# Moving four convolution projections ahead of the third mixer's sigmoid tiles, with a later start of that mixer's chain

## What is computed

```
fc = heads(f_c, H_C)
kc = (1.0 - lbh) * jax.nn.sigmoid(-fc)
log_f = jnp.log1p(-jnp.minimum(kc, GATE_CLAMP))
hC, Sh1 = _gla_chunked(jax.nn.silu(heads(q_c, H_C)), kc, heads(i_c, H_C), log_f, Sh0)
yC = jax.nn.silu(g_c) * _head_rms(hC, norm_c)
yconv, buf1 = _short_conv(cg_d * x_d, buf0, conv_w)
yD = bg_d * yconv
```

## Time and profile before

| | us |
|---|---|
| median of 3 runs | 1595.56 (1595.1 to 1599.61) |
| the profiled execution's own time | 1595.64 |
| its span, first to last instruction | 1593.8 |
| PE busy | 1538.8 (97%) |
| POOL, DVE and ACT busy | 888.1, 996.3 and 666.0 |

### The profile page before, as it was taken

How to read it: one execution, slowest core, us unless ns; L and a number is a source line. 1 busy time by engine, 2 the same in 40 slices (tenths; PEclk the granted TensorE clock), 3 DMA queues, 4 the chain that set the end, 5 groups by cost and what they waited for, 6 DMA issues and landing times.

```text
span 1593.8 us, 26238 instructions
## 1 busy us (share of the span) xinstructions
PE 1538.8 (97%) x10442; PEld 1477.8 (93%) x10442; DVE 996.3 (63%) x1929; ACT 666.0 (42%) x1220; POOL 888.1 (56%) x381
## 2 busy tenths in 40 slices
PE   7899999999999999999888999999999999999996
PEld 7899998999999999999888999889999999999996
DVE  4874775237676777754447747752467767777544
ACT  5434443333444544433344444434344445444333
POOL 6456444444445666677654554444444556666674
PEclk9999999999999999999999999999999999999998
DMA  8333353443354444444433334433334444444442
GB/s 284 119 115 123 137 177 101 154 135 122 121 175 151 142 138 148 151 148 151 139 106 106 119 120 164 161 124 132 122 135 141 156 140 141 136 151 150 149 151 79
DMA packets 66257, 223.61 MB, mean 140 GB/s; under 512 B 8024, under 2 KB 12632, under 8 KB 66136
## 3 DMA queue, kind: packets, MB, share of 16 engines
q1 hardware_dynamic: 66136, 221.93, 43.3%
HBM read 206.33 MB, written 15.58 MB: 139 GB/s over the span
## 4 chain that ended last, share of the span: by engine, by line
PE 87%; DVE 7%; ACT 3%; issue 1%; POOL 1%; DMA 0%; DVEq 0%; ACTq 0%
PE gps L1284 25%; PE gps L1286 24%; PE gps L1285 24%; PE xp L1523 2%; PE xp L1525 1%; PE xp L1460 1%; DVE mix L981 1%; PE xp L1438 1%; PE xp L1419 1%; PE xp L1512 1%; PE xp L1429 1%; PE xp L1421 1%; POOL wlo L594 1%; PE xp L1408 1%; ACT whi L615 1%
## 5 line engine op out<-in xcount | busy, mean ns | idle before, releaser
L594 POOL TENSOR_TENSOR wlo<-raw,whi 128x1024 fp32r<-128x1024 f32 x362 | 875.7, 2421 | 687.2 <-ACT whi L615 413.2
L1284 PE MATMUL gps<-xh,whi 128*128 128x320 f32 (+1 forms) x2000 | 643.3, 322 | 29.7 <-DVE zc L854 12.0
L1285 PE MATMUL gps<-xl,whi 128*128 128x320 f32 (+1 forms) x2000 | 625.7, 313 | 0.0
L1286 PE MATMUL gps<-xh,wlo 128*128 128x320 f32 (+1 forms) x2000 | 624.9, 312 | 0.0
L615 ACT ACTIVATE whi<-raw 128x1024 fp32r<-128x1024 f32 x258 | 272.3, 1056 | 348.7 <-PE gps L1286 297.7
L1284 PEld LDWEIGHTS gps<-xh,whi 128*128 128x128 f32 x2000 | 381.3, 191 | 38.5 <-POOL wlo L594 19.3
L1285 PEld LDWEIGHTS gps<-xl,whi 128*128 128x128 f32 x2000 | 382.8, 191 | 3.4 <-issue 0.4
L1286 PEld LDWEIGHTS gps<-xh,wlo 128*128 128x128 f32 x2000 | 382.3, 191 | 0.0
L1284 PE MATMUL gps<-ah,whi 128*128 128x320 f32 x640 | 199.1, 311 | 0.6
L1286 PE MATMUL gps<-ah,wlo 128*128 128x320 f32 x640 | 197.8, 309 | 0.0
L1285 PE MATMUL gps<-al,whi 128*128 128x320 f32 x640 | 197.7, 309 | 0.0
(11 more groups left out here) (299 smaller groups left out, 1893.3 us busy)
## 6 DMA issues: line engine op xcount, KB each, us to landing
raw<-in_w SPq DMA_DIRECT2D x362, 512.0 KB, 3.5
s<-in_st SPq DMA_DIRECT2D x24, 512.0 KB, 4.3
out_ss<-s SPq DMA_DIRECT2D x24, 512.0 KB, 2.7
con<-in_cst SPq DMA_DIRECT2D x4, 526.0 KB, 5.9
out_sp<-pst SPq DMA_DIRECT2D x24, 64.0 KB, 2.6
mix<-in_x SPq DMA_DIRECT2D x4, 320.0 KB, 4.9
out_y<-mix SPq DMA_DIRECT2D x8, 160.0 KB, 1.9
ee<-in_cst SPq DMA_DIRECT2D x1, 224.0 KB, 4.4
```

What stands on the lines that cost most here:

```text
L594: nc.gpsimd.tensor_tensor(wlo[:, c % RING, :, :], raw[:, c % RING, :, :], whi[:, c % RING, :, :].bitcast(F32), ALU.subtract).then_inc(lo_d ...
L1284: M(out, hi, xhi, start=start, stop=False)
L1285: M(out, hi, xlo, start=False, stop=False)
L1286: return M(out, lo, xhi, start=False, stop=stop)
```

## The change

The four `cD` slots move from places 16 to 19 to places 4 to 7, and `fC`, `qC` and `gC` come four slots later (8 to 19); the packed weights follow the same list, so the DMAs move with them. All stages that are due by those slots move by four: `c_log` 12, 13; `c_first` 16 to 19; `c_level` 21, 23, 25, 27, 29, 31; `c_last` 33. The cost entry of `c_last` falls from 4 to 2, so that `num` follows it by two slots and not by four: `num` 35, 38, 41, 44 and `fin` 36, 39, 42. `fin` of the last head is placed ahead of slot 45, behind slot 44, where `num` of that head and `conv` of head 3 stand too, in the order `num`, `conv`, `fin`. `conv` keeps its slots, and so does everything from slot 45 on.

```
-    for kind in ("vC", "fC", "qC", "gC", "cD", "xD", "bD", "vA", "qA", "kA", "oA", "ifA"):
+    for kind in ("vC", "cD", "fC", "qC", "gC", "xD", "bD", "vA", "qA", "kA", "oA", "ifA"):
...
-COST = {"c_log": 1, "c_first": 1, "c_level": 2, "c_last": 4, "a_gate": 1, "a_cum": 1, "a_row": 2, "a_exp": 1,
+COST = {"c_log": 1, "c_first": 1, "c_level": 2, "c_last": 2, "a_gate": 1, "a_cum": 1, "a_row": 2, "a_exp": 1,
```

## The result

The changed kernel takes 1606.83 us (median of 5 runs, 1603.73 to 1609.74), the kernel before beside it 1595.56 (5 runs, 1595.08 to 1599.61). The ratio is 1.0065, 95% interval 1.0045 to 1.0085: slower by 0.65%, a small loss, but the interval leaves out one. The profiled execution took 1605.67, its span is 1603.9 us against 1593.8, 10.1 longer.

A forecast was written before the change was run, and what follows sets the result against it. PE, busy 1538.8 of 1593.8 us, was taken as the bound. 2 x (0.7 + 2.7 + 1.6) - 0.3 = +9.7 us on 1595.64 gave 1605.3, range 1599 to 1612.

The forecast's parts named there:

- The sigmoid run: Twelve sigmoid tiles in a row, four slots later: cost unchanged, save 0.3 us gained at layer 0's first gap.
- Levels 0 and 1: Slots beside these levels become `xD`, taken out by DVE: distances end late, +0.7 us a layer.
- `c_last` to `num`: `c_last`'s 9.86 us chain covered by two slots, 7.2 us, instead of four: PE waits 2.7 us a layer.
- The tail: Behind slot 44, `num`, `conv`, `fin` without slots between: +1.6 us a layer, including `a_cum`'s wait gone, -1.2.
- `num` to `fin`: Behind slot 44, `fin`'s matmuls wait for `num`'s last copies and `vm`: PE waits about 1.8 us a layer.
- `a_gate`: Behind slot 45, waits for all of `fin`, which ends 4.67 us into a slot covering 3.8: about 1.0 us a layer.
- SP's queue: Stores of `fin` and of head 3's `conv` ahead of slot 49's weights, needed four slots later: cost nothing.
- Clock: Two gaps removed, six added, about two drawing a lower-clock stretch: taken as zero, 3 us either way.
- the first (a meeting of `conv`): `conv` behind slot 44 meets POOL once: +4.2 us for both layers; with one more slow stretch, 1611; chance 0.14.
- the second (L1003 misses POOL): `c_last`'s last DVE product, L1003, does not meet POOL: 1601.1 us; chance 0.10.
- the third: Sigmoid run keeps ahead of PE; all 12.0 us of waits and a slow stretch go: 1591.8 us; chance 0.04.
- the fourth: DVE's chain behind `c_last` and in the tail shorter than bounded, all terms at low ends: 1598 us; chance 0.06.

The follow-up runs named there:

- the exchange: Changed kernel with `c_last`'s two last DVE products swapped, so the one `num` reads comes first: 1601.44 us, ratio 1.0019 to the kernel before.
- e2_cost_only: Kernel before, in its old order of projections, with only the cost of `c_last` lowered from 4 to 2: 1613.08 us, ratio 1.0098.
- e9_one_slot: Changed kernel with the cost of `c_last` at 1 instead of 2, one covering slot before `num`: 1633.07 us, ratio 1.0225 to the kernel before.
- e6_gate_late: Kernel before, costs kept, with `gC` moved behind `qA` and `c_first` beside `cD`: 1586.15 us, ratio 0.9941.
- e3_spread: Changed kernel with `c_last` cost 3 and `finC` cost 1, spreading `num` and `fin` evenly: 1599.47 us, ratio 1.001 to the kernel before.

## Why the prediction was right, and where it was off

1605.3 was forecast and 1606.83 came, in the range and with the sign. By its own steps, measured on the trace:

- **The sigmoid run** (-0.3 for both layers): held. The gaps 2.04, 0.83, 1.83, 1.81 came back four slots later, and layer 0's first one went from 2.37 to 2.04. With the gap that moved from L1453, the term is -0.4.
- **Levels 0 and 1** (+0.7 a layer): 0.2. Both copies met POOL as the step had it, but they were done sooner: the distances began 4.79 us after POOL did, where the step had 5.0 to 5.3, and the first took 0.68 instead of 0.8. So level 0 ended only some 0.2 us late. DVE around it, and POOL:

```profile
99.28 2.07 DVE L908 COPY ud<-cbs 128x16 f32<-128x16 f32 x1
101.86 1.85 DVE L908 COPY ud<-cbs 128x16 f32<-128x16 f32 x1
...
103.75 0.68 DVE L928 TENSOR_TENSOR mix<-zc 128x512 f32<-128x512 f32 x1
...
98.96 4.71 POOL L594 TENSOR_TENSOR wlo<-raw,whi 128x1024 fp32r<-128x1024 f32 x2 [2.60 <-ACT whi L615]
```

- **`c_last` to `num`** (+2.7): 2.70 and 2.69. The wait is chain less cover. It is so at one slot as well (6.22), and the exchange showed the meeting with POOL in it.
- **The tail**: `num` to `fin` +1.8 (its own rows give 160.78 less 159.11, 1.67), measured 1.71 in both layers; `a_gate` +1.0, measured 0.94 in layer 1 and hidden in layer 0; `a_cum` -1.2, gone in both. `conv` was harmless where it stands, as the step assumed. But the two experiments that moved it or left it alone say that this was one good place between bad ones.
- **SP's queue** ("they cost nothing"): this step failed in layer 0, 1.07 us. It looked at the weights of slot 49. Those that came late are slot 47's, behind the stores of `fin` of head 2, and the split of them on ACT stood ahead of the copy that L1438 reads. The timelines of SP's queue and of ACT, layer 0:

```profile
210.13 1.25 SPq L554 DMA_DIRECT2D out_sp<-pst  x1
211.44 0.45 SPq L535 DMA_DIRECT2D raw<-in_w  x1
...
215.76 1.06 ACT L615 ACTIVATE whi<-raw 128x1024 fp32r<-128x1024 f32 x1 [2.38 <-DMA raw<-in_w]
```

  In layer 1 the same store held the queue 0.43 us and not 1.25, ACT waited 1.26 and PE not at all. This is read from the trace; no run moved that load.
- **Clock** (zero, 3 us either way): +1.9 us of PE's busy time. Which gap draws a slow stretch is not the same in two layers: `num`'s did in layer 0 and not in layer 1 with the same 2.7 us.

The sum by what was measured: -0.4 + 0.4 + 5.4 + 3.4 + 0.9 - 2.4 + 1.0 + 1.9 = 10.2, against a span 10.1 longer; forecast were 9.7. Two misses, levels too dear by 1.0 and `a_gate` by 1.1 since layer 0 hid it, were made up by SP's queue and the clock. So the nearness of the total to the forecast is in part luck; the three terms that carry it (L1429, L1512, `a_cum`) are not.

Of the rivals, the first (a meeting of `conv`) didn't come in the change but came in two experiments; the second (L1003 misses POOL) is what the exchange made, and the wait fell by the 2.1 a layer that it names; that its 1601.44 us lies so near the 1601.1 worked out is partly chance, as the kernel before took 2.5 us more beside it and other waits fell too; the third stayed out in the change: its gaps went only when `c_first` left the sigmoid tiles. For the fourth, all terms at their low ends, only the levels came out low (its 0.7 for the tail is less than the step's own bounds give, 1.2 + 1.0 - 1.2).

## What to carry to other kernels

The cost of a stage in a slot scheduler is the length of its chain up to the instruction that the next stage reads, waits for POOL included; it can be read from one trace, and each slot taken from under it comes back as a gap of one slot (6.22 less 2.70 is 3.52, a bare slot 3.54). The time of the whole kernel can't be read so: in `e2_cost_only` and `e9_one_slot` that wait came as forecast and the total missed by some 13 and 22 us (against the kernel before beside each), because stages further on met POOL or late weights in their new places, and because more of the slots ran at the lower clock. When two results leave an engine one after the other, let that come first which the next stage reads. Moving a run of tiles as a whole changed its gaps by only 0.4 us here; what helped was to put DVE's chain beside tiles that another engine takes out (`e6_gate_late`). And with every stage that moves, look at the weights which stand behind its stores, not only at the nearest ones by name.

## What was not expected of the hardware

- The same kernel's span follows the mean granted clock: of `e3_spread` one execution spans 1594.9 us at 0.987 and another 1602.7 at 0.982, with the same instructions; of the kernel before, 1593.2 at 0.987 and 1600.8 at 0.982. A stretch at the lower level began at the end of a gap of 2.70 us in layer 0 (165.90), and none at that of 2.69 in layer 1. What decides it was not settled, and it sets how finely a change here can be measured.
- More gaps cost more than themselves: from the change to `e9_one_slot`, PE's idle time grows by 17.3 us and its busy time by 10.6, at a mean clock of 0.975 instead of 0.985.
- A copy of 16 columns on DVE (L908) takes 1.85 to 2.07 us while POOL works from SBUF, and 0.16 when POOL rests (105.53 in the kernel before). It loses as much as a large product: the price is POOL's remaining time and not the size of the copy. The copy has one input and meets POOL all the same, so the prediction's rule, which speaks of two inputs in SBUF, is too narrow.
